# A two-layer block on one core: x transposed raw in four pieces, the first norm's root applied after the first products, vectors loaded as columns

## What is computed

```python
def rmsnorm(x, g):
    y = xf * lax.rsqrt(jnp.mean(xf * xf, axis=-1, keepdims=True) + NORM_EPS)
    return (y * g)
...
def mla_mixer(h, positions, w_in, q_norm, w_uq, kv_norm, w_ukv):     # h = rmsnorm(x, layer_norm[0])
    proj = h @ w_in                                                   # 2048 -> 512 + 512 + 64 + 2048
    c_q, c_kv, k_rope, gate = jnp.split(proj, ...)
    q = (rmsnorm(c_q, q_norm) @ w_uq)          # 16 heads, 128 nope + 64 rope each
    kv = (rmsnorm(c_kv, kv_norm) @ w_ukv)      # 16 heads, 128 k_nope + 128 v each
    k_rope = rope(k_rope, positions)
    y = mla_causal_attention(q_nope, q_rope, k_nope, k_rope, v)
    return y, gate
...
x = x + (y * jax.nn.silu(gate)) @ w_out
```

## Time and profile before

| | |
|---|---|
| median of three runs | 1817.72 us |
| the profiled execution | 1817.26 us |
| its span (first to last instruction) | 1815.5 us |
| PE busy | 1789.0 us (99%) |
| DVE busy | 1139.9 us (63%) |
| ACT busy | 896.6 us (49%) |
| POOL busy | 151.9 us (8%) |
| granted TensorE clock, mean | 0.999 |

### The profile page before, as it was taken

How to read it: one execution, slowest core, us unless ns; L and a number is a source line. 1 busy time by engine, 2 the same in 40 slices (tenths; PEclk the granted TensorE clock), 3 DMA queues, 4 the chain that set the end, 5 groups by cost and what they waited for, 6 DMA issues and landing times.

```text
span 1815.5 us, 35122 instructions
## 1 busy us (share of the span) xinstructions
PE 1789.0 (99%) x13046; PEld 1669.7 (92%) x13046; DVE 1139.9 (63%) x1795; ACT 896.6 (49%) x1351; POOL 151.9 (8%) x186
## 2 busy tenths in 40 slices
PE   6999999999999999999999999999999999999998
PEld 5999998899999878999999889999999999988886
DVE  6665655656777766775565666666666666644445
ACT  6555454545554555554444546455544544433333
POOL 1001110000101101000000000100000000033321
PEclk9999999999999999999999999999999999999999
DMA  7655555566445456665565656666566666666554
GB/s 234 166 170 147 161 156 174 183 179 185 151 141 165 150 186 181 180 200 171 170 174 156 210 161 202 194 195 185 186 196 189 195 194 196 197 196 195 189 194 139
DMA packets 235612, 326.46 MB, mean 180 GB/s; under 512 B 12432, under 2 KB 170420, under 8 KB 234896
## 3 DMA queue, kind: packets, MB, share of 16 engines
q1 hardware_dynamic: 233440, 318.61, 56.9%
q0 software_dynamic: 1808, 6.69, 1.3%
q10 hardware_dynamic: 288, 0.11, 0.0%
HBM read 323.24 MB, written 2.13 MB: 179 GB/s over the span
## 4 chain that ended last, share of the span: by engine, by line
PE 97%; DVE 1%; ACT 1%; DMA 1%; issue 0%; POOL 0%; ACTq 0%; POOLq 0%; DVEq 0%; SPq 0%
PE bank L509 17%; PE bank L511 17%; PE bank L510 17%; PE bank L517 8%; PE bank L518 8%; PE bank L519 8%; PE bank L1140 3%; PE bank L1138 3%; PE bank L1139 3%; PE scores L544 3%; PE bank L544 2%; PE bank L547 1%; PE scores L1140 1%; PE scores L1138 1%; PE scores L1139 1%; PE scores L547 1%
## 5 line engine op out<-in xcount | busy, mean ns | idle before, releaser
L1690 DVE TENSOR_TENSOR w_low<-raw,w_high 128x1024 fp32r<-128x1024 f32 x603 | 735.5, 1230 | 557.4 <-ACT w_high L1179 555.9
L1179 ACT CAST w_high<-raw 128x1024 fp32r<-128x1024 f32 x603 | 626.7, 1049 | 630.5 <-PE bank L511 319.0
L509 PE MATMUL bank<-hT_high,w_high 128*128 128x256 f32 x2608 | 728.3, 279 | 0.7 <-DVE hT_low L1707 0.3
L510 PE MATMUL bank<-hT_low,w_high 128*128 128x256 f32 x2608 | 722.2, 277 | 0.0
L511 PE MATMUL bank<-hT_high,w_low 128*128 128x256 f32 x2608 | 722.2, 277 | 0.0
L509 PEld LDWEIGHTS bank<-hT_high,w_high 128*128 128x128 f32 x2608 | 490.0, 188 | 7.7 <-issue 6.9
L511 PEld LDWEIGHTS bank<-hT_high,w_low 128*128 128x128 f32 x2608 | 489.8, 188 | 0.0
L510 PEld LDWEIGHTS bank<-hT_low,w_high 128*128 128x128 f32 x2608 | 489.7, 188 | 0.1
L517 PE MATMUL bank<-w_high,yT_high 128*128 128x512 f32 x384 | 152.2, 396 | 0.4 <-POOL yT_low L2511 0.4
L519 PE MATMUL bank<-w_high,yT_low 128*128 128x512 f32 x384 | 149.8, 390 | 0.0
L518 PE MATMUL bank<-w_low,yT_high 128*128 128x512 f32 x384 | 149.7, 390 | 0.0
(11 more groups left out here) (327 smaller groups left out, 2121.6 us busy)
## 6 DMA issues: line engine op xcount, KB each, us to landing
raw<-in_w_up SPq DMA_DIRECT2D x176, 512.0 KB, 4.5
raw<-in_w_in SPq DMA_DIRECT2D x88, 512.0 KB, 3.8
raw<-in_w_down SPq DMA_DIRECT2D x88, 512.0 KB, 4.4
raw<-in_w_swa SPq DMA_DIRECT2D x72, 512.0 KB, 3.9
raw<-in_w_c SPq DMA_DIRECT2D x50, 512.0 KB, 3.9
raw<-in_w_mlao SPq DMA_DIRECT2D x32, 512.0 KB, 3.8
raw<-in_w_swao SPq DMA_DIRECT2D x32, 512.0 KB, 4.5
raw<-in_w_out SPq DMA_DIRECT2D x32, 512.0 KB, 4.3
```

What stands on the lines that cost most here:

```text
L509: nc.tensor.matmul(to, h, act_h[:, chunk, :], start=first, stop=False, skip_group_check=True)
L510: nc.tensor.matmul(to, h, act_l[:, chunk, :], start=False, stop=False, skip_group_check=True)
L1179: nc.scalar.copy(whi(tile, i, n), raw[s][:, :]).then_inc(high_made, 1)
L1690: v.tensor_tensor(wlo(tile, i, n), raw[s][:, :], whi(tile, i, n).bitcast(F32), ALU.subtract).then_inc(low_made, 1)
```

## The change

- x is loaded in four pieces of 512 columns of both halves of the tokens, 512 KB each, each ahead of two weight tiles in SP's queue. The constants without the identity move behind the eighth weight tile.
- PE transposes raw x (`turn_first`) in four pieces, eight blocks each, between the weight tiles of the first group: ahead of tiles 0, 1, 3 and 5. Ahead of the first piece stand 12, behind it 20 transposes of the identity whose result is not used (`warm`).
- The normed copy `nx` of x, `normalise0` and `normalise1`, are gone. The squares of x are taken by ACT after eleven weight tiles' casts; the roots go onto c_sb (`first_rows_out`), and by two matmuls with a diagonal of roots into a row `r_mla`, which is multiplied onto k_rope and onto each pair's gates (`gate_in`).
- The gate leaves bank 0 by `gate_in` into SBUF; tanh and `gate_out` work there in the next step, and PE waits for `gate_in`.
- The vectors are laid out as columns by the host and come in two loads: slot 0 on ACT's queue, the others on POOL's after the last piece of x. The six transposes and their copies are gone.

```diff
-TURN_BANKS = (tuple(range(8)), ...
+TURN_BANKS = ((4, 5, 6, 7, 2, 3, 4, 5), ...
@@ sync
-            for t in range(TT):
-                sp.dma_start(x[:, t, :], a["x"][t * P:(t + 1) * P, :]).then_inc(x_in[t], 16)
-            for j in range(2):
-                load(T_C + j, wv["w_c"][:, 2 * j:2 * j + 2, 0:512])
-            sp.dma_start(cst[:, P:], a["constants"][:, P:]).then_inc(consts_in, 16)
+                sp.dma_start(x[:, :, cols], x_rows[:, :, cols]).then_inc(x_in[g], 16)
             for g in range(2):
                 for j in range(8):
+                    if g == 0 and j % 2 == 0:
+                        load_x(j // 2)
+                    load(T_C + 8 * g + j, wv["w_c"][:, 2 * j:2 * j + 2, g * 512:(g + 1) * 512])
+                if g == 0:
+                    sp.dma_start(cst[:, P:], a["constants"][:, P:]).then_inc(consts_in, 16)
@@ tensor
+            def turn_first(g):
+                pe.wait_ge(x_in[g], 16)
+                if g == 3:
+                    pe.wait_ge(hl_done, 2)
+                for b in (2 * g, 2 * g + 1):
+                    to = banks[TURN_BANKS[0][b]]
                     for c in range(2):
                         for t in range(TT):
-                            last = flip(banks[b][:, c * SEQ + t * P:c * SEQ + (t + 1) * P],
-                                        nx[:, t, (2 * b + c) * P:(2 * b + c + 1) * P])
+                            last = flip(to[:, c * SEQ + t * P:c * SEQ + (t + 1) * P],
+                                        x[:, t, (2 * b + c) * P:(2 * b + c + 1) * P])
                     last.then_inc(tr_done, 1)
...
-            pe.wait_ge(rows_in_act, 16 * (N_ROWS // 2))
-            pe.wait_ge(rows_in, 16 * (N_ROWS - N_ROWS // 2))
...
-            pe.wait_ge(cols_done, 1)
-            transpose_rows()
+            warm(12)
+            turn_first(0)
+            warm(20)
+            first_tile(0, 0)
+            turn_first(1)
+            first_tile(0, 1)
+            first_tile(0, 2)
+            turn_first(2)
+            first_tile(0, 3)
+            first_tile(0, 4)
+            turn_first(3)
+            for j in range(5, 8):
+                first_tile(0, j)
+            for j in range(8):
+                first_tile(1, j)
+            pe.wait_ge(first_diag_done, 1)
+            for t in range(TT):
+                last = f32mm(banks[6][:, t * P:(t + 1) * P], first_ones, first_diag[:, t, :])
+            last.then_inc(first_r_psum, 1)
@@ scalar
+            act.wait_ge(first_cols_in, 16)
+            for b, tiles in ((0, (-3,)), (1, (-2,)), (2, ()), (3, (-1, 0)), (4, ()), (5, (1, 2)), (6, ()), (7, range(3, 8))):
+                banks_high(0, V_LN0, b)
+                for t in tiles:
+                    split(T_C + t)
@@ mla_step of scalar and vector
                 else:
                     tile(0)
+                    gate_tanh(i - 1)
...
                     tile(1)
+                    gate_out(i - 1)
...
                 tile(6, 7)
                 if project:
-                    gate_out(i)
+                    gate_in(i, T_MLA + 8 + i * 8)
@@ vector
+            for b, tiles in ((0, (-3,)), (1, (-2,)), (2, ()), (3, (-1, 0)), (4, ()), (5, (1, 2)), (6, ()), (7, range(3, 10))):
+                banks_low(0, V_LN0, b)
+                for t in tiles:
+                    split(T_C + t)
+            def gate_in(i, used, bank=banks[0]):
+                dve.wait_ge(tiles_used, used)
+                after(dve, ml["y32_done"], i)
+                v.tensor_tensor(gate[:, 0:2, :], bank.rearrange("p (h n) -> p h n", h=2), over(r_mla, 2),
+                                ALU.mult).then_inc(ml["gate_in"], 1)
```

More of the change, by code:

```diff
@@ L1317, in _, with gate_tanh @@
                 last.then_inc(c_hh, 1)
[L1319 to L1323 removed]
+            def gate_tanh(i):
+                after(act, ml["gate_in"], i + 1)
+                after(act, ml["gate"], i)
+                nc.scalar.activation(gtan[:, 0:2, :], gate[:, 0:2, :], ACT.Tanh, scale=0.5).then_inc(ml["tanh"], 1)
             split(T_MLA + 2)
             split(T_MLA + 3)
[L1327 removed]
             act.wait_ge(kr_done, 1)
```

182 lines of the change are left out of this document (77 added, 105 removed).

## The result

| | before | after |
|---|---|---|
| median (lowest to highest), 20 runs each | 1817.64 us (1816.49 to 1818.92) | 1819.95 us (1818.80 to 1821.13) |
| the profiled execution | 1817.26 us | 1820.94 us |
| its span | 1815.5 us | 1819.0 us |

The ratio is 1.0013, 95% interval 1.0007 to 1.0019: the kernel is 2.3 us slower. That is under the 0.2% that the prediction calls no change, but the interval leaves out 1.0, so slower it is. The time lies in the range of the prediction; the sum said 0.85 us faster, and 2.3 us slower has the other sign.

What follows compares the result with a forecast made beforehand. PE, busy for 99% of the span, was taken as the bound. Tile 0 starting 7.25 us earlier, less 6.4 us given back, made -0.85 us, so 1816.9 us against the median, with a range of 1814.0 to 1820.4.

Steps and rivals of the forecast that it cites:

- Identity lands at 6.0: Kernel start: the identity's load, issued at 1.88, lands at 6.0 us, with ends of 4.5 and 9.9.
- Rival 3: Kernel start: the identity lands as late as before, +3.9 us on the forecast, 1820.8 us; chance 0.08.
- From the identity to tile 0: Kernel start: warming, first blocks, table load, evictions, cast and low part take from 6.0 to 14.35 us.
- 24 transposes, 2.6: First weight tiles: the three later pieces of x put 24 transposes between tiles, 0.11 each, giving back 2.6 us.
- Holes, 1.1 each: Ahead of tiles 2, 4 and 6: PE waits 1.1 us each for evictions, cast and low part, 3.3 us together.
- Root matmuls, 0.5: Two matmuls that make the row of roots cost PE 0.5 us, between 0.2 and 0.9.
- Late low part of tile 15, 0: First group's end: DVE's low part is ready just when PE wants it, 0 to 1.5 us, taken as 0.
- The MLA loop at nothing: Seven loop steps: the moved gate work and table load fit into idle time and room, costing zero.
- rival 2: MLA loop: the table load lands on the path, +9.0 us over seven steps, 1825.9 us; chance 0.05.
- Rival 4: Ahead of tile 0: PE falls back to the slow pace in a 1.8 us hole, +2.1, 1819.0 us; chance 0.10.
- The untouched rest at nothing: Everything outside the start and the MLA loop: untouched by the change, so no term in the sum.

Runs made afterwards that it cites:

- table_early: The changed kernel with a dummy activation ahead of ACT's first wait, so that the table load runs there: 1818.47 us, ratio 1.0005.
- after_less_code: The changed kernel with 8 warming transposes in place of 32, 48 instructions fewer on PE: 1820.67 us, ratio 1.0015.
- warm_behind: The changed kernel with the 12 warming transposes ahead of the first piece of x moved behind it: 1818.40 us, ratio 1.0005.
- before_more_code: The kernel before with 32 more instructions on PE, waits for what is long done, in idle time ahead of the identity: 1818.88 us, ratio 1.0007.
- before_again: The kernel before, unchanged, run and traced once more as a control: 1817.71 us, ratio 1.0000.
- ident_first: The changed kernel with the identity's load moved from ACT's queue to the head of SP's: 1815.40 us, ratio 0.9990.
- before_columns: The kernel before with only the vectors as columns in two loads, their six transposes and copies gone: 1816.64 us, ratio 0.9996.
- together: The changed kernel with early table load, identity and slot 0's columns on SP's queue, casts ahead of evictions, 16 and 14 warming transposes: 1811.59 us, ratio 0.9969.

## Why the prediction was right or wrong

- **Identity lands at 6.0**: wrong, and this is the step that failed. It landed at 8.5, inside the ends of 4.5 and 9.9, but the value was taken near the lower one. That is +2.5 us, and with it the sign. The reason given was that 0.5 MB of x goes ahead where 2 MB went, so that "most of what stood before it is gone". That count left out the weight tiles: with them 1.5 MB were issued ahead of the identity in after, and 2.5 MB in before (x at 0.74 and 1.19, a weight tile at 1.66). This took only 1.4 us off (8.0 to 6.6 from issue), while the head of SP's queue takes 4.7 more off. Rival 3 (the identity as late as before, its wait coming from the queue) named a cause of this kind, at 3.9; the runs do not part the queue from the order of issue.
- **From the identity to tile 0**: right. 8.35 us predicted (6.0 to 14.35), 8.24 measured (8.51 to 16.75). The table load was on the path by 1.28, as read from the order, and table_early shows it. The eviction starts 0.01 us after the load's end (12.28 + 1.28 = 13.56; it starts at 13.57). By the Trainium skill (ScalarE: Activation LUTs, "What ACT_TABLE_LOAD costs") a drain of 1.38 stands beside the load; this trace shows none.
- **24 transposes, 2.6**: 2.7. **Holes, 1.1 each**: 1.03, in the three predicted places and for the predicted reason. **Root matmuls, 0.5**: 0.46, as the rest of the sum to 1.41 and not measured by itself. **Late low part of tile 15, 0**: no hole there; from 45 to 100 us PE's only wait is the 0.8 ahead of the scores, as in before.
- **The MLA loop at nothing**: right, and rival 2 is out. ACT in one step of after, answering to the earlier trace rows:

```profile
120.07 1.28 ACT L1198 ACT_TABLE_LOAD   x1
121.83 1.05 ACT L1198 CAST w_high<-raw 128x1024 fp32r<-128x1024 f32 x1 [0.47 <-PE bank L513]
...
125.89 0.40 ACT L1270 ACTIVATE prob<-prob,neg_max 128x128 f32<-128x128 f32 x1 [2.49 <-DVE neg_max L1756]
```

The load fills the idle time and leaves 0.47 of it. Behind it the exponentials start 1.32 later than before, less than PE's 1.41. DVE's last scaling of probabilities, moved back by `gate_out`, and PE's use of them, answering to the earlier trace rows:

```profile
129.87 0.68 DVE L1883 SCALAR_TENSOR_TENSOR gate<-gate_tanh,gate 128x512 f32<-128x512 f32 x1
131.34 0.35 DVE L1772 TENSOR_SCALAR prob<-prob,row_rcp 128x256 f32<-128x256 f32 x1
```

```profile
134.07 0.49 PE L549 MATMUL bank<-constants,prob 128*128 128x128 f32 x3
```

They end at 131.69, 2.4 us ahead of PE: of 2.9 us of room 0.5 was used.

- **Rival 4, the slow pace behind the hole**: out for after, whose hole ahead of tile 0 is 1.18 us and not 1.8: its next matmuls start at 17.06, 17.29 and 17.52, at 0.23 each. after_less_code does not test it, since PE was still slow ahead of its hole; its 1.9 us are the price of too little warming, where 2.1 was put on a lost pace. The mechanism itself is real and shows at another place, the roots of the FFN in warm_behind, with the granted clock at 0.50 behind a wait of 1.99 us. That agrees with the Trainium skill (TensorE: Matmul & The Clock Gate, "HAM oscillation — how this bites in real kernels"), that a wait for data can put PE's clock back.
- **The untouched rest at nothing**: wrong, by 0.75 as far as the medians tell. No step of the prediction had it: "All the rest of the kernel is untouched but for the MLA loop" was taken to mean that it takes as long. It looked at what each instruction waits for, and not at where in PE's program it stands.

With both errors put in, -0.85 + 2.4 (tile 0 at 16.75, not 14.35) - 0.1 (the three small terms) + 0.75 = +2.2; measured +2.3. The 0.75 was itself taken from the measured difference, so what this confirms is the start: +1.45 by the corrected sum, 1.41 in the traces, 1.56 in the medians without the hole.

That the time still lies in the range is in part luck. The range reached up to 1820.4 for rival 4 and the near end of rival 3; 1819.95 got there by a late identity and a term at nothing.

What stays open: whether the identity is late by its queue or by the order of issue; the rest of after's longer wait at the roots (1.2 in after_less_code against 0.4 to 0.6); and how the fetch delays the weight tile. That the two meet is read from the DMA records and fits before_more_code; no run moved the fetch alone to other places. The records also have a second kind of fetch, in blocks of 8 KB. One falls into the tile's transfer in after and in after_less_code and none does in before_again or ident_first; but before_columns has one there and waits 0.6, and together has none and waits 2.2.

## What to carry to other kernels

When PE is 99% busy, what it waits for at the start is paid in full. Put the small load that everything waits for at the head of the queue of the large ones, ahead of them; here that gave 4.5 us. When you count what stands ahead of a load, count every load issued before it, not only those of the same tensor. Look in the order for what the compiler has put behind the first wait (here a table load) and move it ahead with a dummy. And look in the whole kernel for places where an engine's program has work for later ahead of work for now: here such a place cost from 0.4 to 2.2 us, by edits 1100 us away, and turning the two about gained 0.8, 1.6 and 2.3 us in three versions.

## What was not expected of the hardware

- A load of 64 KB on ACT's queue, issued at 1.88 us, took 6.6 us with three loads of 512 KB issued ahead of it on SP's queue, and 8.0 with two of 1 MB and one of 512 KB; issued at 0.74 at the head of SP's queue it took 1.9. ACT's queue moved its first packet only 3.7 us after the issue (at 5.62), SP's after 1.1.
- With the vectors in two loads in place of twelve, of about as many bytes, the second half of x came not earlier but 1.5 us later (before_columns).
- 32 more instructions on PE that do nothing, in idle time, put 0.6 to 0.8 us on a wait 1100 us behind them. A block of PE's program is 16 KB and takes 0.9 us or more in the DMA records (in before 0.88 to 1.56, half of them under 0.96).
- A wait of 1.99 us at the roots put the granted clock to 0.50 for 3.4 us in one traced execution; one of 1.91 us at the same place in another kernel did not.
